# An order of steps for each engine in the attention stage of a decoder layer

## The chip, the cores and the metric

The kernel runs on one core of a Trainium2 chip, in one launch. Its engines work side by side, each through its own list of instructions: TensorE (PE, matmuls and transposes into PSUM), VectorE (DVE), ScalarE (ACT), GpSimd (POOL) and SyncE (SP), which starts most DMAs. They meet at semaphores: an instruction waits until a counter has reached a value, and everything behind it on the same engine waits too. The metric is the device time of the whole execution in microseconds.

## What is computed

One step of a two-layer decoder over 1024 prompt tokens and 8 x 4 sampled tokens. The first layer has a convolution branch and a sparse attention; the change lies in the attention. Cut to it:

```
def nsa_block(q, g, q_pos, kc, vc, kc_end, ks, vs, kw, vw, kw_pos):
    s_c = einsum('bqhgd,bnhd->bhgqn', qg, kc)          # compressed keys
    o_c = einsum(..., masked_softmax(s_c, ...), vc)
    ...                                                # scores of blocks, the best 16 are chosen
    s_s = einsum('bqhgd,bhqnd->bhgqn', qg, k_sel)      # selected keys
    o_s = einsum(..., masked_softmax(s_s, ...), v_sel)
    s_w = einsum('bqhgd,bwhd->bhgqw', qg, kw)          # window of 512 keys
    o_w = einsum(..., masked_softmax(s_w, ...), vw)
    return g0 * o_c + g1 * o_s + g2 * o_w
```

The prompt has 8 query tiles of 128 tokens and 2 key-value groups of 4 heads. For the samples the same is done over 2048 cached keys each, which are gathered from pages.

## The kernel before

**Units, pairs and turns.** The prompt's attention is cut into 48 units (query tile, group, branch), branch being PRS (selected), PRW (window) or PRC (compressed). Each unit has two pairs of heads, so 96 pairs. A pair goes through five steps on four engines: S, the scores (PE, L1137, 64 to 1024 keys, two rows of PSUM banks out of four); the row minimum with the mask (DVE, L1228, one instruction for each row); E, the exponential (ACT, L1177); the reciprocal of its sum (DVE, L1224); C, the scaling by that and by the gate (POOL, L1382). Then the unit's probabilities, 128 keys at a time, make 148 turns: T, four transposes into a PSUM bank (PE, L1151); a copy to one of two PT buffers (DVE L1165 or ACT L1168); V, the values (PE, L1024), which add up in bank 6. When a unit group of three branches is done, DVE multiplies it out (O, L1329).

**Work around them.** H is one of four subtractions of XL for the convolution half (DVE, L1334). The samples go through one PSUM bank, bank 7, in a chain of their own: scores over the compressed keys, a ranking of blocks (DVE, three steps for each of two halves, L1261 to L1269), and then, for each of four groups of two samples, gathers of keys (POOL, L1367), five rounds of key transposes (PE L1067, copied by ACT to KTS) and scores (PE L1072), two exponentials (ACT, L1191), two scalings (POOL, L1390), probability transposes (PE L1087 to L1092) and values (PE L1113). Each filling of bank 7 waits until the one before it has been taken out. The next group's gathers and window loads wait for the last values of a group. The loads of the output weights (SP, WOR) wait for the values of the last group; ACT rounds them (L1558) and POOL and DVE make the low part (L1562, L1570) before the output projection (PE, L1602).

**What sets the order.** One list, ORDER, is made by a loop that walks through the S and T steps with a rough clock, puts each E one S or T later and each C two later, and drops the sample steps in at given distances. Every engine walks through this one list and does what in it is its own. On PE the values of a turn come right behind the next S or T (flush). Copies are shared by the turn's number: even to DVE, odd to ACT. The steps H, the first gathers and the preparation (prep) are inserted at fixed places.

## Time and profile before

| | us |
|---|---|
| median of 3 runs | 1255.46 (1255.13 to 1256.18) |
| the profiled execution | 1259.05 |
| its span in the trace | 1257.3 |
| PE busy in the span | 1166.9 |
| DVE, ACT, POOL busy in the span | 751.5, 380.9, 330.7 |

A row of the trace gives the start, the duration, the engine, the line, what is written and read, and, in brackets, how long the engine stood idle before it and which instruction of which engine released it. The granted clock of PE is given as a share of 2.4 GHz; it knows two levels, 1.2 and 2.4 GHz, so 0.75 over a stretch means half of it at each.

### The profile page before, as it was taken

The page shows a single profiled execution, that of the slowest core. Times are in us where ns is not written, and L with a number is a line of the kernel's source. Part 1 is how long each engine was busy: PE and PEld are TensorE (multiplying, and loading weights), DVE is VectorE, ACT ScalarE, POOL GpSimd, SP SyncE. Part 2 cuts the span into 40 slices and gives each one's busy share as a digit, 9 for nine tenths or more (in the row PEclk, how much of TensorE's full clock was granted, in tenths as well). Part 3 has the DMA queues.
Part 4 walks back from the last instruction along what each step waited for, and adds up shares of the span by engine and source line. Part 5 has one row for each costly group of instructions (what it writes and reads, how often), then busy time and mean ns, then how long its engine had stood idle before and what let it go on. Part 6 is the DMA issues. An engine that isn't in the chain of part 4 may idle for free.

```text
span 1257.3 us, 17799 instructions
## 1 busy us (share of the span) xinstructions
PE 1166.9 (93%) x7124; PEld 939.9 (75%) x7124; DVE 751.5 (60%) x1381; ACT 380.9 (30%) x805; POOL 330.7 (26%) x340
## 2 busy tenths in 40 slices
PE   5888999999999688998999999889999999989997
PEld 4878999999889444554544545478879999988884
DVE  3566899998854686455355454484555660157555
ACT  3112111223124445545345455441011221234000
POOL 3443510000005654342333333340002221216000
PEclk9999999999999689799799999999999999999999
DMA  7553511433200400040040400272212111131221
GB/s 229 182 163 120 169 50 34 137 122 97 55 17 1 177 1 1 2 167 1 2 167 1 168 1 11 92 200 84 88 56 84 35 48 33 40 134 68 101 101 42
DMA packets 78011, 103.17 MB, mean 82 GB/s; under 512 B 21248, under 2 KB 64392, under 8 KB 76831
## 3 DMA queue, kind: packets, MB, share of 16 engines
q1 hardware_dynamic: 69839, 67.52, 17.3%
q0 software_dynamic: 6016, 33.56, 7.0%
q10 hardware_dynamic: 2080, 1.05, 0.3%
q8 instruction: 51, 0.84, 0.3%
q14 instruction: 25, 0.20, 0.1%
HBM read 90.42 MB, written 16.64 MB: 85 GB/s over the span
## 4 chain that ended last, share of the span: by engine, by line
PE 82%; DVE 8%; ACT 5%; issue 3%; POOL 2%; DMA 1%; SPq 0%; ACTq 0%; POOLq 0%
PE PS L681 24%; PE PS L1602 15%; PE PS L1764 14%; PE PS L1137 6%; PE PS L1024 5%; PE PS L1151 4%; PE PS L673 3%; PE PS L1113 2%; PE PS L1072 2%; DVE ACC L548 2%; PE PS L1067 1%; ACT PRW L1177 1%; PE PS L1744 1%; DVE PS L1228 1%; ACT PRS L1177 1%
## 5 line engine op out<-in xcount | busy, mean ns | idle before, releaser
L681 PE MATMUL PS<-XH,WH 128*128 128x352 f32 (+1 forms) x648 | 148.3, 333 | 3.1 <-DVE XL L523 3.1
L595 DVE SCALAR_TENSOR_TENSOR Y<-U,SM,Y 128x1024 f32<-128x1024 f32 x120 | 147.4, 1291 | 0.3
L681 PE MATMUL PS<-XH,WL 128*128 128x352 f32 (+1 forms) x648 | 143.0, 325 | 0.0
L681 PE MATMUL PS<-XL,WH 128*128 128x352 f32 (+1 forms) x648 | 142.9, 325 | 0.0
L681 PEld LDWEIGHTS PS<-XH,WH 128*128 128x128 f32 (+1 forms) x648 | 108.3, 187 | 6.5 <-DVE XL L523 3.8
L681 PEld LDWEIGHTS PS<-XL,WH 128*128 128x128 f32 (+1 forms) x648 | 109.8, 187 | 1.4
L681 PEld LDWEIGHTS PS<-XH,WL 128*128 128x128 f32 (+1 forms) x648 | 109.8, 186 | 1.4
L1024 PE MATMUL PS<-PT,TM 128*64 128x256 f32 x528 | 91.8, 428 | 12.2 <-ACT PT L1168 6.0
L548 DVE SCALAR_TENSOR_TENSOR ACC<-PS,SM,ACC 128x508 f32<-128x508 f32 x124 | 84.0, 739 | 30.7 <-PE PS L673 29.9
L1602 PE MATMUL PS<-WOH,XH 128*128 128x512 f32 (+1 forms) x288 | 91.4, 399 | 4.9 <-POOL WOL L1570 4.4
L1228 DVE CUSTOM_DVE_ANT_0 PS<-PS,MASKC 128x128 f32<-128x128 f32 (+7 forms) x96 | 62.6, 692 | 55.8 <-PE PS L1137 55.5
L1871 POOL TENSOR_TENSOR WL<-WRAW,WH 128x1024 fp32r<-128x1024 f32 x14 | 37.4, 2674 | 220.2 <-ACT WH L1816 220.2
L1137 PE MATMUL PS<-KV,Q 64*128 64x512 f32 (+3 forms) x384 | 87.3, 515 | 6.1 <-ACT PRS L1177 3.1
L290 POOL TENSOR_TENSOR WL<-WRAW,WH 128x1024 fp32r<-128x1024 f32 x12 | 28.6, 2386 | 244.4 <-ACT WH L362 244.4
L1602 PE MATMUL PS<-WOL,XH 128*128 128x512 f32 (+1 forms) x288 | 89.7, 393 | 0.0
L1602 PE MATMUL PS<-WOH,XL 128*128 128x512 f32 (+1 forms) x288 | 89.3, 391 | 0.0
L1382 POOL TENSOR_SCALAR PRS<-PRS,STAT,GTOK 128x128 f32<-128x128 f32 (+7 forms) x64 | 55.5, 878 | 96.5 <-DVE STAT L1224 96.3
L1165 DVE COPY PT<-PS 128x512 f32<-128x512 f32 x74 | 51.0, 689 | 50.1 <-PE PS L1151 49.3
L1764 PE MATMUL PS<-XH,WH 128*128 128x352 f32 x360 | 77.2, 323 | 0.0
L1764 PE MATMUL PS<-XH,WL 128*128 128x352 f32 x360 | 77.1, 323 | 0.0
L1764 PE MATMUL PS<-XL,WH 128*128 128x352 f32 x360 | 77.1, 323 | 0.0
L1137 PEld LDWEIGHTS PS<-KV,Q 64*128 64x128 f32 x384 | 38.9, 198 | 47.9 <-issue 26.1
(315 smaller groups left out, 2070.2 us busy)
## 6 DMA issues: line engine op xcount, KB each, us to landing
WRAW<-in_w_in_even SPq DMA_DIRECT2D x16, 512.0 KB
WRAW<-in_w_in_odd SPq DMA_DIRECT2D x16, 512.0 KB, 4.0
XIN<-in_x_prompt SPq DMA_DIRECT2D x8, 512.0 KB, 12.8
WRAW<-in_w_in_even SPq DMA_DIRECT2D x16, 256.0 KB
TM<-in_state_win_kv SPq DMA_DIRECT2D x8, 512.0 KB, 4.6
XR<-in_x_prompt SPq DMA_DIRECT2D x8, 512.0 KB, 3.5
layer_out<-R SPq DMA_DIRECT2D x8, 512.0 KB, 2.6
XR<-layer_out SPq DMA_DIRECT2D x8, 512.0 KB, 3.3
```

Of the source, the lines that this page charges most:

```text
L548: ins = v.scalar_tensor_tensor(acc, rows, weight, acc, ALU.mult, ALU.add)
L595: v.scalar_tensor_tensor(dst, src, CWT[:, i, t:t + 1], dst, ALU.mult, ALU.add).then_inc(s_cv, 1)
L673: ins = pe.transpose(PS[:, 6 + x, b * P:b * P + P], XC[:, load % 2, b, 256 * j + P * x:256 * j + P * x + P], ident[:, :])
L681: ins = pe.matmul(PS[0:mcols, 3 * slot + c, 0:CH], w[:, slot, kk, 0:mcols], x[:, kk, c * CH:(c + 1) * CH], start=(kk == 0 and n == 0), sto ...
L1024: ins = pe.matmul(PS[hb:hb + HD, 6, 256 * gp:256 * gp + 256], v, PT[0:rows, t % 2, 256 * h:256 * h + 256], start=first, stop=(br == CMPB))
L1137: ins = pe.matmul(PS[:, row_bank[j] + b // 512, 0:w], Q[hb:hb + HD, g, tok(qt)], keys[:, k0 + b:k0 + b + w], start=True, stop=True)
L1151: ins = pe.transpose(PS[0:cols, 4 + t % 2, c:c + P], probs(u, 2 * gl + h, i * P, cols), ident[:, :])
L1165: copy(PT[0:rows, t % 2, :], PS[0:rows, 4 + t % 2, :]).then_inc(sem, 1)
L1228: return v.tensor_tensor_reduce(out=out, in0=in0, in1=mask, scale=-SCALE, scalar=1e27, op0=ALU.add, op1=ALU.min, accum_out=acc)
L1382: po.tensor_scalar(x, x, RCP[:, stat(p, h):stat(p, h) + 1], GTOK[:, qt, c:c + 1], ALU.mult, ALU.mult)\
L1602: ins = pe.matmul(PS[0:n, b0 + hf, :], x[:, kk, tok(tt)], w[:, kk, hf * 512:hf * 512 + 512], start=(kk == 0 and i == 0), stop=(kk == KT - ...
L1764: ins = pe.matmul(PS[:, b0 + c, 0:CH], w[:, slot, kk, :], x[:, kk, c * CH:(c + 1) * CH], start=(kk == 0 and n == 0), stop=(kk == KT - 1 an ...
```

## The change

The list ORDER goes. Every step is declared with its engine, a kind, a duration in ns and the steps whose outputs it needs, and a planner lets simulated engines run: it takes again and again the step that can begin first, at equal times by the engine's order of kinds (URGENT), and appends it to that engine's own list.

```diff
-        for n, x in enumerate([("H", i) for i in range(4)] + [("gather", 0), ("prep",)]):
-            ORDER.insert(FIRST_H + 2 * n, x)
...
+        for p in range(NP):
+            u, n = p // 2, nkeys(p // 2)
+            step("PE", "S", ("S", p), 100 + 3.44 * n, *{("E", w // 2, w % 2) for w in row_waits[2 * p:2 * p + 2] if w >= 0})
+            for h in range(2):
+                step("DVE", "M", ("M", p, h), 180 + 1.13 * n, ("S", p))
+                step("ACT", "E", ("E", p, h), 250 + 0.84 * n, ("M", p, h), ("T", unit_last_turn[u - 3]) if u >= 3 else None)
+            step("DVE", "R", ("R", p), 170 if UNITS[u][2] != CMPB else 450, ("E", p, 1))
+            step("POOL", "C", ("C", p), 660 + 1.7 * n, ("R", p))
+        for t, (u, i) in enumerate(TURNS):
+            step("PE", "T", ("T", t), 520, ("C", 2 * u), ("C", 2 * u + 1), ("P", t - 2) if t >= 2 else None)
+            step("PE", "V", ("V", t), 550, ("P", t), ("O", u // 3 - 1) if u % 3 == 0 and i == 0 and u else None)
...
+            for k in range(3):
+                step("ACT", "X", ("sexp", gi, k), 1100 if k < 2 else 920, ("low", gi))
...
+            for k in range(2):
+                step("POOL", "X", ("sscale", gi, k), 810 if k else 2080, ("srec", gi))
...
+        URGENT = {"PE": "XSVT", "DVE": "PRMOQXH", "ACT": "PEX", "POOL": "CX"}
+        HANDOVER = 130
...
+            if kind == "T":
+                free = {c: max(now[c], end[what]) + ns * (1 + len(copies[c])) for c, ns in (("DVE", 690), ("ACT", 600))}
+                copier.append(min(("ACT", "DVE"), key=free.get))
+                copies[copier[-1]].append(what[1])
...
-            return (s_pted, t // 2 + 1) if t % 2 == 0 else (s_ptea, t // 2 + 1)
+            return s_pted if copier[t] == "DVE" else s_ptea, copier[:t + 1].count(copier[t])
...
+                    elif n == 1:
                         link(v.tensor_tensor(RE[:, :, :], RE[:, :, :], LT[:, :, :], ALU.mult))
-                    elif n == 1:
+                    elif n == 2:
                         link(v.tensor_tensor(RG[:, :, :], other, me, ALU.is_gt))
+                    elif n == 3:
                         link(v.tensor_tensor(RG[:, :, :], RG[:, :, :], RE[:, :, :], ALU.add))
...
-                    for i, t in enumerate((SS, SW)):
-                        act.activation(t[r, :], t[r, :], ACT.Exp, bias=ENM[r, 2 + i:3 + i], scale=-1.0,
-                                       accum_out=EDN[r, 2 + i:3 + i]).then_inc(s_eex, 1)
+                    half = (PAST + NSAMP) // 2
+                    t, i, total = ((SS[r, 0:half], 2, EDN[r, 2:3]), (SS[r, half:], 2, EDN2[r, :]), (SW[r, :], 3, EDN[r, 3:4]))[k]
+                    act.activation(t, t, ACT.Exp, bias=ENM[r, i:i + 1], scale=-1.0, accum_out=total).then_inc(s_eex, 1)
...
+                    link(v.tensor_tensor(EDN[r, 2:3], EDN[r, 2:3], EDN2[r, :], ALU.add))
```

So the minimum and the exponential of a pair's two rows become single steps; the values of a turn are a step of their own; a turn's copy goes to the engine that the planner finds free first, which gives DVE 49 and ACT 99 of the 148; the ranking has six steps for each half; the long exponential of a sample group is split in two, with an addition of the two sums; the two scalings of a group are two steps; and the four parts of a group's values stand one behind the other on PE. The first group's keys are taken 10 score steps and 9 turns later than before, and the last values of the last group come five turns before the end (turn 143 of 148, before 128).

At the start of the stage on DVE (ISA with MASKC is the minimum over a score row, XL the H step). Before:

```order
L1228 ISA PS,STAT<-PS,MASKC 128x128
L1228 ISA STAT 128x1
L1334 TENSOR_TENSOR XL<-Y,XH 128x1056 x2
L1224 RECIPROCAL STAT<-STAT 128x2
L1334 TENSOR_TENSOR XL<-Y,XH 128x1056
L1228 ISA PS,STAT<-PS,MASKC 128x128
```

After, at the same place:

```order
L1252 ISA PS,STAT<-PS,MASKC 128x128
L1252 ISA STAT 128x1
L1359 TENSOR_TENSOR XL<-Y,XH 128x1056
L1248 RECIPROCAL STAT<-STAT 128x2 x2
L1252 ISA PS,STAT<-PS,MASKC 128x128
```

Two H steps stood ahead of the first reciprocal, behind six score rows; now one stands ahead of the first two, behind four.

The start of the stage on POOL, from the last work of the convolution (XH) on. Before:

```order
L350 CAST XH<-Y 128x1056 x4
L1382 TENSOR_SCALAR PRS<-PRS,STAT,GTOK 128x128 x2
L1367 DMA RING<-in_cache_kv_sel,idx 128x4096 x2
L1382 TENSOR_SCALAR PRS<-PRS,STAT,GTOK 128x128 x2
L1432 IOTA TI 128x4
L1433 IOTA TI 128x1
L1435 MEMSET NEWM 128x64
L1436 AFFINE_SELECT NEWM<-NEWM 128x64
L1438 AFFINE_SELECT NEWM<-NEWM 128x64
L1440 MEMSET LT 128x900
L1441 AFFINE_SELECT LT<-LT 128x900
L1382 TENSOR_SCALAR PRW<-PRW,STAT,GTOK 128x128 x4
```

After:

```order
L350 CAST XH<-Y 128x1056 x4
L1409 TENSOR_SCALAR PRS<-PRS,STAT,GTOK 128x128 x4
L1409 TENSOR_SCALAR PRW<-PRW,STAT,GTOK 128x128 x4
L1409 TENSOR_SCALAR PRC<-PRC,STAT,GTOK 128x63 x4
L1409 TENSOR_SCALAR PRS<-PRS,STAT,GTOK 128x128 x4
L1409 TENSOR_SCALAR PRW<-PRW,STAT,GTOK 128x128 x4
L1394 DMA RING<-in_cache_kv_sel,idx 128x4096 x2
```

The gathers moved behind ten pairs, and the preparation (IOTA to the second LT row) behind fourteen.

ACT around the exponentials of the first sample group (SS, SW; PT is a turn's copy). Before:

```order
L1168 ACTIVATE PT<-PS 128x512
L1177 ACTIVATE PRS,STAT<-PS,STAT 128x512 x2
L1191 ACTIVATE SS,SE<-SS,SE 64x2080
L1191 ACTIVATE SW,SE<-SW,SE 64x544
L1168 ACTIVATE PT<-PS 63x512
L1177 ACTIVATE PRS,STAT<-PS,STAT 128x512 x2
```

After:

```order
L1195 ACTIVATE PT<-PS 128x512
L1202 ACTIVATE PRC,STAT<-PS,STAT 128x63
L1217 ACTIVATE SS,SE<-SS,SE 64x1040
L1195 ACTIVATE PT<-PS 128x512
L1217 ACTIVATE SS,SE<-SS,SE 64x1040
L1217 ACTIVATE SW,SE<-SW,SE 64x544
L1202 ACTIVATE PRS,STAT<-PS,STAT 128x640
```

A turn's copy now stands between the two halves of the long one in this group.

## Rows read from the trace of the kernel before

**Rows 1.** The page, second part: PE's granted clock in 40 slices, in tenths.

```profile
PEclk9999999999999689799799999999999999999999
```

**Rows 2.** Stretches: bounds, length, busy time of PE, PEld, DVE, ACT, POOL, clock, DMA.

```profile
410.68:816.05 405.37, 361.45 (x2449) 199.51 (x2448) 217.77 (x722) 195.84 (x539) 157.54 (x219) 0.92 0.16 61
410.68:436.87 26.19, 16.07 (x93) 10.39 (x92) 16.36 (x68) 10.68 (x48) 18.68 (x31) 0.61 0.56 213
410.68:500.00 89.32, 70.33 (x405) 38.73 (x406) 64.33 (x251) 44.61 (x168) 50.19 (x82) 0.81 0.17 63
500.00:816.05 316.05, 291.12 (x2046) 160.78 (x2042) 153.43 (x471) 151.22 (x371) 107.35 (x138) 0.95 0.16 61
```

**Rows 3.** Waits of PE in the stage: total, times, longest.

```profile
PE PS L1137 <- ACT PRW L1177: 8.6, 7, 3.1
PE PS L1024 <- DVE PT L1165: 6.9, 7, 1.5
PE PS L1024 <- ACT PT L1168: 6.8, 21, 1.7
PE PS L1072 <- ACT KTS L1168: 6.0, 15, 0.9
```

**Rows 4.** Timeline of PE: two turns' transposes at the lower clock and at full.

```profile
462.78 1.97 PE L1151 MATMUL PS<-ident,PRS 128*128 128x128 f32 x8
...
799.18 1.09 PE L1151 MATMUL PS<-ident,PRS 128*128 128x128 f32 x8
```

**Rows 5.** Stretches as in rows 2: those with a lowered clock, and the rest.

```profile
410.68:450.00 39.32, 27.98 (x151) 16.97 (x150) 26.22 (x125) 18.71 (x84) 25.51 (x45) 0.65 0.37 142
460.00:470.00 10.00, 8.34 (x35) 4.49 (x34) 7.60 (x29) 4.04 (x17) 5.52 (x8) 0.66 0.00 1
510.00:530.00 20.00, 19.23 (x100) 11.03 (x98) 8.37 (x32) 11.38 (x31) 10.46 (x14) 0.67 0.01 1
600.00:620.00 20.00, 18.14 (x105) 11.54 (x107) 5.19 (x22) 6.90 (x22) 7.91 (x10) 0.57 0.00 1
620.00:816.05 196.05, 182.78 (x1348) 100.51 (x1343) 98.79 (x283) 95.15 (x223) 65.87 (x80) 1.00 0.18 71
```

**Rows 6.** Timeline of PE: the first transposes of the first two turns.

```profile
424.25 1.11 PE L1151 MATMUL PS<-ident,PRS 128*128 128x128 f32 x4 [3.40 <-POOL PRS L1382]
...
429.28 1.12 PE L1151 MATMUL PS<-ident,PRW 128*128 128x128 f32 x4 [1.28 <-POOL PRW L1382]
```

**Rows 7.** Timeline of DVE and POOL at the start of the stage.

```profile
415.36 2.42 DVE L1334 TENSOR_TENSOR XL<-Y,XH 128x1056 fp32r<-128x1056 f32 x2
...
417.96 2.88 POOL L1382 TENSOR_SCALAR PRS<-PRS,STAT,GTOK 128x128 f32<-128x128 f32 x2 [3.04 <-DVE STAT L1224]
...
423.32 0.88 POOL L1382 TENSOR_SCALAR PRS<-PRS,STAT,GTOK 128x128 f32<-128x128 f32 x2
```

**Rows 8.** Timeline: a rank step of DVE, and the values of PE behind it.

```profile
456.15 1.33 DVE L1265 TENSOR_TENSOR RG<-RG,RE 128x900 f32<-128x900 f32 x1
...
459.05 0.65 PE L1024 MATMUL PS<-PT,VC 63*64 63x256 f32 x4 [0.86 <-DVE PT L1165]
```

**Rows 9.** Timeline: the second group's long exponential, and PE behind it.

```profile
591.76 2.02 ACT L1191 ACTIVATE SS<-SS,SE 64x2080 f32<-64x2080 f32 x1 [1.59 <-DVE SE L1277]
...
595.28 0.65 PE L1024 MATMUL PS<-PT,TM 128*64 128x256 f32 x4 [1.74 <-ACT PT L1168]
```

**Rows 10.** Last sample values, the loads behind them (KB, us to landing), the projection's start.

```profile
783.18 0.41 PE L1113 MATMUL PS<-VCN,TM 127*32 127x128 f32 x4
...
WOR<-in_w_out_even SPq DMA_DIRECT2D x4, 512.0 KB, 6.4
...
818.87 0.70 PE L1602 MATMUL PS<-WOH,XH 128*128 128x512 f32 x2 [2.82 <-POOL WOL L1570]
```

**Rows 11.** The gathers' line: from issue to landing.

```profile
DMA to landing us min/median/max: 8.9/11.5/14.6
```

**Rows 12.** Timeline of PE: a score step over 1024 keys.

```profile
785.73 1.99 PE L1137 MATMUL PS<-KV,Q 64*128 64x512 f32 x8
```

261 lines of the change are left out of this document (129 added, 132 removed).

## The prediction

> **What bounds the kernel now.** I read the page first, its busy rows in forty slices. TensorE (PE) is the fullest engine nearly everywhere, and its granted clock dips in only one part, slices 14 to 20 [rows 1]. That part is the attention stage, the only one that the change touches. The table by stretches gives its size: from the first scores at 410.68 to the last values at 816.05 it lasts 405.37 us, with PE busy for 361.45 us and idle for 43.9 us. DVE, ACT and POOL are busy for 217.77, 195.84 and 157.54 us of it, so none of them bounds the stage as a whole [rows 2]. The waits of PE in the stage name what it stood for: copies by ACT and DVE, mostly short (21 waits make 6.8 us), and exponentials in fewer and longer waits [rows 3].
>
> Busy time is not all work. The eight transpose records of two turns take 1.09 us at full clock and 1.97 us at the lower level of 1.2 GHz [rows 4], 1.81 times as long, so of what is done at the lower level 0.447 is excess. The mean clock in a stretch says how much of it lay at the lower level: 0.65 means 70%. Taken so, 19.6 us of the busy time up to 450, 5.7 us in 460 to 470, 12.7 us in 510 to 530 and 15.6 us in 600 to 620 were run at 1.2 GHz, and from 620 to the end none [rows 5]. That is 53.6 us, with 24.0 us of excess. So the stage is 337.4 us of PE work, 24.0 us of slow clock and 43.9 us of idling. Only the last two can go: the floor is 68 us below today's time.
>
> **The change, part by part.** The instructions stay the same but for four groups of small ones (below); what changes is who waits behind whom. Before, one list orders all engines; after, each has its own.
>
> *The start.* The first turn's transposes start at 424.25, after a wait of 3.4 us, and the second turn's at 429.28 [rows 6]. The chain behind them is on other engines: DVE subtracts two rows of XL (2.42 us from 415.36) before the first reciprocal, POOL then scales the first pair in 2.88 us instead of the 0.88 of the next, issues two gathers up to 423.3, scales the second pair and runs the preparation of the masks before the third [rows 7]. After, DVE has one XL row of half of 2.42 us before the first two reciprocals, and the gathers come behind ten pairs on POOL. That XL row can start about 1.1 us before today's 415.36, since two of the six score rows ahead of it, for which PE was waited, now stand behind (an estimate); it then ends at 415.5, the reciprocals at 415.8, four scalings of 0.44 us at 417.7; the next two pairs, one round of the same steps later, are scaled by about 420. So the first turn starts 6.4 us earlier and the second 9 us; I take **-7**, ends -5.5 and -9. What hides the rest of the XL rows is that nothing on PE needs them before the output projection, except through the gathers.
>
> The row of 2.88 us is POOL beside a DVE subtraction with both inputs in SBUF: 1.0 us lost for each scaling. From rows alone, POOL is idle for 248 of the stage's 405 us [rows 2] and the same instructions collide before and after, so I take 0 for such collisions, with +3 as an end. The Trainium skill, SBUF — State Buffer, section "Who interferes with whom", says that such a DVE instruction and a GpSimd one that reads SBUF exclude each other and that the second waits in full. By that rule, the trace agrees; and it speaks against the change, since three XL rows and eight of the twelve rank steps now stand among POOL's scalings, so that POOL would lose up to the length of each.
>
> *Rank steps.* DVE ran them in pairs. The second half of one, 1.33 us, ends at 457.5; the copy behind it is late and PE's values wait 0.86 us [rows 8]. After, each half stands alone. Between 436.87 and 500 PE idles 19.0 - 10.1 = 8.9 us [rows 2]. The early part also has DVE 72% busy (64.33 of 89.32 us), and the free choice of the copier takes 25 of DVE's 74 copies away, for ACT with 44.61 us busy [rows 2]. I take **-4** of the 8.9, ends -2 and -7.
>
> *Exponentials of the samples.* ACT was held by one of 2.02 us and a shorter one right behind; a copy due meanwhile came late, and PE's values waited 1.74 us [rows 9]. After, a copy or a pair's exponential can stand between three pieces of half that length. Of the 24.9 us of idling after 500 (316.05 - 291.12) I put 4 us on this: one such wait for each of four groups, less where PE had other work, and part of the 8.6 us for ACT's PRW, which stands behind the same block. The remaining waits are the short ones. With only half a turn between a turn's transposes and its values, the copy and its handovers are some 0.3 us too long (6.8 us in 21 waits). In the new order I count 18 turns with just one such piece between, against 27 before, so these shrink by a third; the waits between sample steps (6.0 us for L1072) keep their kind. With what the better places of the other copies bring I take -5 here, so **-9** after 500, ends -4 and -14.
>
> *Clock.* The two drops after 500 each come behind a block of ACT by the exponentials of a sample group (the second is the one shown), while from 620 on, with PE 93% busy, the clock stayed at full [rows 5]. Their excess is 0.447 x (12.7 + 15.6) = 12.7 us; I take **-10**, ends 0 and -12.7. The early excess is 0.447 x (19.6 + 5.7) = 11.3 us; the fill at the start stays, shorter by a third, so I take **-5.5**, ends 0 and -9.
>
> *Added.* Four more exponentials and four additions on DVE of a few hundred ns each (an estimate from the 0.44 us of the shortest scalings): they lie on the sample chain, which PE meets only at its end. **+0.5**, ends 0 and +2.
>
> *End of the stage.* The loads of the output weights wait for the last sample values. These ended at 783.6, 32 us before the stage's end; now some eleven pieces of 0.55 us and a wait or two follow, about 7 us. The loads land 6.4 us after their issue in the median, and ACT wants the first one some 6.3 us after it, when its last copy is done. They are just hidden: 0, with +2 as an end. The wait of 2.82 us at the start of the output projection stays [rows 10].
>
> *Gathers.* A sample group's gathers land after 8.9 to 14.6 us [rows 11]. Between its predecessor's last values and its first use stand five score steps (up to 2.0 us each) and 14 halves of turns, 12 to 15 us: covered, or short by 1 to 2 us in two or three groups, which is inside the ends above.
>
> The sum is -7 - 4 - 9 - 10 - 5.5 + 0.5 = **-35 us** against the profiled execution's 1259.05 us, so 1224. The median of the runs is 3.6 us lower than the profiled one, 1255.46, so I predict **1220 us**. With all favourable ends the sum is -52; the poor one (-5.5, -2, -4, a third of the clock, +2) is -15: its own range is 1204 to 1240.
>
> **Rivals.** (1) *The waits go, the clock stays low as long as before.* All of -19.5 comes, nothing of -15.5: 1236. For it: the start remains a fill, and 18 short waits remain. Against it: 620 to 816 has 13 us of idling in short waits and a clock of 1.00 throughout [rows 5]. The Trainium skill has a rule for this, TensorE: Matmul & The Clock Gate, section "A second HAM failure mode: psum-queue depth-cycling": frequent short idling between groups of matmuls makes the clock go to and fro.
>
> (2) *The planned order is wrong in detail.* Its table prices a score step at 3.44 ns per key and pair, 3.6 us for 1024 keys; the row shows 1.99 us [rows 12]. Engines keep their order however early a step's input is there, so a copy planned behind an exponential may come late, and each saved wait returns elsewhere. Then only the start and the split exponentials are left, about -10: 1245. Against it: between two wide score steps PE must wait for both exponentials anyway, about 4.2 us, and the planner leaves as much for other work.
>
> (3) *Slower: short waits everywhere bring the clock down.* Same mechanism as (1), going further: turns now come as two transposes and two values, with about 0.3 us of idling in a pair. It decides from the point where the busy time at 1.2 GHz passes 53.6 + 19.5/0.447 = 97 us. With a third of the 337 us of work there, it takes 0.81 x 112 = 91 us longer than at full clock, where today's excess is 24; less the 19.5 us of waits that is 48 us slower, about 1303. Against it is again the stretch from 620, where such pairs stand already.
>
> **Chances.** Forecast 0.74, (1) 0.12, (2) 0.06, (3) 0.06, no change for unseen reasons 0.02. A measurement tells about 0.2% (2.5 us) from no change. Faster 0.91, same 0.03, slower 0.06. The range reaches over (1) and half of (2): 1203 to 1243, with some 2 in 10 outside.
>
> **What would show it.** First transposes at about 418 and second at 420; the stage some 370 us long with at most 25 us of PE idling; the clock at 1.00 from about 440 on, with no drop at the sample exponentials; DVE with about 49 copies. It would be wrong if the clock stays below 0.95 over the stage, if PE waits more for copies than 14 us in all, or if the output projection starts more than 4 us behind the last values.

## The result, and the profile after

The kernel after takes 1201.39 us (median of 4 runs, 1198.82 to 1204.59) against 1255.30 us before (4 runs, 1250.78 to 1256.18): ratio 0.958, 95% interval 0.9549 to 0.9611. The direction was as forecast; the size was not. The forecast was -35 us, and it came out as -54, beyond the lower end of the range at 1203. The profiled executions, 1259.05 and 1204.59 us, differ by 54.5 us.

The page of the kernel after, second part: PE's granted clock in 40 slices (before: rows 1).

```profile
PEclk9899999999999979999999999899999999999999
```

One lowered slice is left in the stage; a slice is 30 us. The stage runs from the first scores at 412.64 to the last values at 762.35. The view by stretches has the columns of rows 2.

```profile
412.64:762.35 349.71, 330.08 (x2449) 191.88 (x2448) 203.44 (x701) 208.61 (x572) 158.08 (x219) 0.98 0.18 68
412.64:500.64 88.00, 78.68 (x483) 44.19 (x482) 69.95 (x284) 55.77 (x205) 59.03 (x95) 0.90 0.18 64
500.64:762.35 261.71, 251.40 (x1970) 147.69 (x1966) 133.49 (x417) 152.83 (x367) 99.05 (x125) 1.00 0.18 69
762.35:1202.90 440.55, 422.29 (x2258) 375.06 (x2256) 228.90 (x296) 88.90 (x138) 78.34 (x29) 0.98 0.26 82
```

Against [rows 2] the stage is 55.7 us shorter. What follows it takes 440.55 us; before it was 1257.3 - 816.05 = 441.25. What lies ahead of it ended 2.0 us later. So the whole difference is in the stage: -55.7 + 2.0 - 0.7 = -54.4 us, as the spans say. The same number of matmuls, 2449, stands in both stages.

The stage can be cut into three, as the prediction did, here with the clock of each slice of 10 us for both kernels: idle time, the low clock's excess (0.447 of what was run at the lower level), and the rest, which I call **work at full clock**.

| stage, us | length | idle | excess of the low clock | work at full clock |
|---|---|---|---|---|
| before | 405.4 | 43.9 | 23.8 | 337.7 |
| after | 349.7 | 19.6 | 6.8 | 323.3 |
| difference | -55.7 | -24.3 | -17.0 | **-14.4** |
| forecast | -35 | -20 | -15.5 | 0 |

The forecast's -35 has 0.5 us more for the added instructions. Idle time and clock are near the forecast. The last column is what was missed: with the same instructions, PE was busy for 14 us less, clock apart. The waits of PE that are left (total, times, longest; before: rows 3):

```profile
PE PS L1056 <- ACT PT L1195: 7.8, 17, 1.2
PE PS L1165 <- ACT PRW L1202: 3.3, 5, 1.2
PE PS L1179 <- POOL PRS L1409: 1.8, 2, 0.9
PE PS L1094 <- DMA RING<-in_cache_kv_sel,idx: 1.5, 2, 0.9
PE PS L1069 <- DVE QBD L1441: 1.2, 1, 1.2
PE PS L1056 <- DVE BG L1354: 1.0, 2, 0.6
PE PS L1056 <- DVE PT L1192: 0.9, 4, 0.3
```

No wait is over 1.2 us, where [rows 3] had one of 3.1 us. The largest total is now that of values (L1056) for a turn's copy by ACT; before it was that of scores for the exponentials.

### The profile page after: what moved, and what is told of

Same layout as the page of the kernel before. It is cut to its first block, busy times and chain, and to the rows that moved or that the text cites. A ratio compares the mean times of both kernels' runs of the same rounds, so it can differ in the third digit from the quotient of the medians.

```text
span 1202.9 us, 17825 instructions
## 1 busy us (share of the span) xinstructions
PE 1138.5 (95%) x7124; PEld 934.8 (78%) x7124; DVE 734.9 (61%) x1360; ACT 394.8 (33%) x838; POOL 330.4 (27%) x340
## 4 chain that ended last, share of the span: by engine, by line
PE 83%; DVE 8%; DMA 4%; ACT 3%; POOL 1%; issue 1%; SPq 0%; ACTq 0%; POOLq 0%; DVEq 0%
PE PS L681 25%; PE PS L1629 17%; PE PS L1791 14%; PE PS L1165 5%; PE PS L1056 5%; PE PS L1179 4%; PE PS L673 3%; DMA RING<-in_cache_kv_sel,idx 2%; PE PS L1140 2%; PE PS L1094 2%; DVE ACC L548 2%; PE PS L1099 2%; DVE PS L1252 1%; PE PS L1771 1%; DMA idx<-in_page_table 1%
## 5 line engine op out<-in xcount | busy, mean ns | idle before, releaser
L1056 PE MATMUL PS<-PT,TM 128*64 128x256 f32 x528 | 82.3, 407 | 9.9 <-ACT PT L1195 7.8
L1165 PE MATMUL PS<-KV,Q 64*128 64x512 f32 (+3 forms) x384 | 78.5, 498 | 0.4 <-ACT PRS L1202 0.3
L1195 ACT ACTIVATE PT<-PS 128x512 f32<-128x512 f32 (+1 forms) x99 | 59.0, 597 | 55.7 <-PE PS L1179 55.4
L1679 DVE SCALAR_TENSOR_TENSOR R<-XR,PS 128x1024 f32<-128x1024 f32 (+1 forms) x18 | 21.9, 1219 | 81.3 <-PE PS L1629 81.3
## 6 DMA issues: line engine op xcount, KB each, us to landing
XIN<-in_x_prompt SPq DMA_DIRECT2D x8, 512.0 KB, 12.7
```

The costliest lines, as they stand in the source:

```text
L1056: ins = pe.matmul(PS[hb:hb + HD, 6, 256 * gp:256 * gp + 256], v, PT[0:rows, t % 2, 256 * h:256 * h + 256], start=first, stop=(br == CMPB))
L1165: ins = pe.matmul(PS[:, row_bank[j] + b // 512, 0:w], Q[hb:hb + HD, g, tok(qt)], keys[:, k0 + b:k0 + b + w], start=True, stop=True)
L1195: copy = lambda o, i: act.activation(o, i, ACT.Copy)
```

## Where busy time hid a wait

A score step (L1137 before) issues the matmuls of two heads in turn. Each head waits inside the step, before its own first matmul, for the exponential that frees its banks. The timeline of PE in the kernel before has these two neighbours:

```profile
596.19 2.12 PE L1137 MATMUL PS<-KV,Q 64*128 64x512 f32 x8 [0.26 <-ACT PRS L1177]
...
600.06 2.12 PE L1137 MATMUL PS<-KV,Q 64*128 64x512 f32 x8 [1.18 <-ACT PRW L1177]
```

Both are steps over 640 keys. Another one over 640 keys, the same eight matmuls, takes less in the same trace:

```profile
792.59 1.35 PE L1137 MATMUL PS<-KV,Q 64*128 64x512 f32 x8
```

A step of 1.35 us has both heads' matmuls side by side; in one of 2.12 us the first head began when its bank was free, and the second came later. The profile names only the wait ahead of the first matmul, and counts what lies between the heads as busy. Single records bear it out: in the steps of 1.35 us the second head's first matmul starts 0.01 us after the first head's, in one of 1.57 us it is 0.23 us, in those of 2.12 us 0.78 us. So the step is longer by about what the second head is late. The reading was tested by putting both waits ahead of the step.

### Both waits ahead of a score step, in before and after

The edit is the same in both kernels:

```diff
                     k0, nk = P * key_tiles(u)[0], nkeys(u)
+                    if max(row_waits[2 * p:2 * p + 2]) >= 0:
+                        pe.wait_ge(s_exp, max(row_waits[2 * p:2 * p + 2]) + 1)
                     for b in range(0, nk, 512):
...
-                            if b == 0 and row_waits[j] >= 0:
-                                pe.wait_ge(s_exp, row_waits[j] + 1)
```

> The kernel before, with one edit: a score step waits for the exponentials that free both of its rows' banks before its first matmul, where before it began the first row as soon as that one's bank was free. Theory A (part of PE's busy time in the kernel before was waiting inside score steps, which the records count as work, since the two heads' matmuls run side by side only when both may start): 640-key steps of 2.12 us turn into 1.35 us with an idle time ahead of them; PE busy in the stage falls by 5 to 8 us, idle rises by as much, the time stays within 3 us of 1255. Theory B (a score step's busy time is work and does not depend on the wait): busy time stays at 361 us within 2, idle rises by the full wait for the second exponential, about 1 us for each of some 20 steps, and the time rises by 10 to 20 us.

Measured: 1259.03 us (1252.57 to 1262.02, 10 runs) against 1255.23, ratio 1.0023 (0.9998 to 1.0049). The stage as a stretch, and its longest waits of PE:

```profile
412.23:819.01 406.78, 352.02 (x2449) 192.69 (x2448) 217.03 (x722) 195.91 (x539) 158.17 (x219) 0.92 0.16 61
```

```profile
PE PS L1137 <- ACT PRW L1177: 14.9, 11, 3.6
PE PS L1137 <- ACT PRS L1177: 8.1, 8, 2.5
```

Busy time fell by 9.4 us and idle time rose by 10.9. The time is 3.8 us up by the medians, which the interval doesn't tell from no change; theory B's 10 to 20 us are excluded. Theory A stands, with more hidden than its 5 to 8 us. The waits of score steps for the exponentials rose from 8.6 us for PRW [rows 3] and 3.1 for PRS to 23.0. So of the 337.7 us of "work" some 9.6 were waiting: 328.1 us are left. Then the same in the kernel after:

> The kernel after, with one edit: a score step waits for the banks of both its rows before its first matmul, as in the same edit of the kernel before, where 9.4 us of TensorE's busy time in the stage turned into idle time. The stage of the kernel after is 349.7 us, 330.1 of it busy, and its busy time less the low clock's excess is 11 to 14 us under that of before. Theory A (before held some 9 us of waiting inside its score steps, and the planned order holds almost none): busy falls by no more than 4 us (to 326 or more), the waits of score steps for the exponentials (3.3 us) rise to at most 8, and the time stays within 4 us, 1199 to 1205. So 5 us or more of the 11 to 14 are these waits gone. Rival (both orders hold as much, and the gain in busy time is all from steps of one kind that stand together): busy falls by 8 to 10 us, to 321, those waits rise to 12 or more, and the time stays as well or rises to 1206 to 1210.

Measured: 1199.75 us (1197.15 to 1200.68, 4 runs) against 1255.98, ratio 0.9545 (0.9507 to 0.9582).

```profile
409.46:756.88 347.42, 323.35 (x2449) 185.16 (x2448) 203.91 (x701) 207.21 (x571) 157.89 (x219) 0.99 0.18 69
```

Work at full clock is 319.9 us, 3.4 less than in after. Waits for exponentials became 4.7 + 3.0 us, from 3.3. So the planned order removed 9.6 - 3.4 = 6.2 us of waiting that the profile of before shows as busy time. The time is like that of after: theory A.

## Steps of one kind together

After the edit above, no score step waits between its heads, and the two orders still differ: 328.1 against 319.9 us, 8.2 us. Rows of the kernel after show what could make this: two turns' values that stand one behind the other, and a single one.

```profile
736.65 0.65 PE L1056 MATMUL PS<-PT,TM 128*64 128x256 f32 x4 [0.35 <-ACT PT L1195]
737.24 1.09 PE L1179 MATMUL PS<-ident,PRS 128*128 128x128 f32 x8
...
740.06 1.08 PE L1056 MATMUL PS<-PT,TM 128*64 128x256 f32 x8
741.08 0.44 PE L1165 MATMUL PS<-KCT,Q 64*128 64x63 f32 x4
```

Rows that follow each other without a wait overlap by some 0.07 us, so it is the starts that count: behind the single one the next row starts after 0.59 us, behind the pair after 1.02. The pair saves 0.15 us against two single ones. The order of after has two values steps together in 32 places (before in 1), two transposes in 38 (27), and its PE changes from one kind of step to another 394 times (451); these are counts of the order of steps, with the samples' steps as one kind.

### Strict alternation, without and with the waits ahead

Values of turn t - 2 must stand ahead of the transposes of t, and transposes of t + 1 ahead of the values of t.

```diff
-            step("PE", "T", ("T", t), 520, ("C", 2 * u), ("C", 2 * u + 1), ("P", t - 2) if t >= 2 else None)
-            step("PE", "V", ("V", t), 550, ("P", t), ("O", u // 3 - 1) if u % 3 == 0 and i == 0 and u else None)
+            step("PE", "T", ("T", t), 520, ("C", 2 * u), ("C", 2 * u + 1), ("V", t - 2) if t >= 2 else None)
+            step("PE", "V", ("V", t), 550, ("P", t), ("T", t + 1) if t + 1 < len(TURNS) else None, ("O", u // 3 - 1) if u % 3 == 0 and i == 0 and u else None)
```

> The changed kernel, but its planner must alternate turns: the values of turn t come behind the transposes of t+1, and the transposes of t+2 behind those values (no two value steps and no two transpose steps stand together; 32 and 38 did). Theory A (each change between transposes and values costs PE 0.06 to 0.07 us, since two together take 1.02 to 1.04 us and a single one 0.58): busy time in the stage rises by 4 to 5 us over the 330 of the changed kernel, waits for copies fall by up to 6, the time is 1198 to 1205. Theory B (PE's work is the same in any order): busy stays at 330 within 1.5, waits fall by 4 to 6 us, the time falls to 1195 or so.

Measured: 1207.19 us (1205.48 to 1208.60, 4 runs) against 1255.23, ratio 0.9615 (0.959 to 0.964). Changes of kind rose to 462.

```profile
412.67:764.98 352.31, 340.24 (x2449) 190.97 (x2448) 188.22 (x672) 224.56 (x601) 156.04 (x219) 0.97 0.18 71
```

Idle time fell to 12.1 us, the lowest of all these kernels, with 0.6 us in waits of values for ACT's copies; and yet the stage is longer than in after, since PE is busy for 10 us more: 7.0 of work at full clock and 3.1 of the low clock's excess. Both theories had the time too low, and theory A had the busy time's rise at 4 to 5 us. This kernel could itself hold more waits inside its score steps, so it was run with these ahead as well.

> The kernel after with two edits: strict alternation of a turn's transposes and an earlier turn's values (alone: 1207.2, busy time less the low clock's excess 331.1 us in the stage, against 324.2 in after), and the waits for the banks of both rows ahead of each score step (alone: 1199.8, 320.5 us). Theory A (the 6.9 us between alternation and after are what changes between kinds of steps cost; the waits inside score steps are about the same few us in both): the edit takes 2 to 5 us out, 326 to 329 us stay, 6 us or more above the 320.5 of after with the same edit; time 1204 to 1209. Rival H (the alternating order holds more waits inside score steps, and changes of kind cost nothing): 9 to 11 us go, 320 to 322 us stay, the waits of score steps for the exponentials rise by as much; time the same or 1 to 3 us up.

Measured: 1205.16 us (1202.78 to 1206.95, 4 runs) against 1258.19, ratio 0.9588 (0.9539 to 0.9637).

```profile
407.49:761.18 353.69, 336.74 (x2449) 185.17 (x2448) 187.06 (x672) 224.82 (x601) 156.01 (x219) 0.97 0.18 70
```

| work at full clock, us | waits inside the steps | waits ahead | changes of kind on PE |
|---|---|---|---|
| before | 337.7 | 328.1 | 451 |
| after, strictly alternating | 330.3 | 327.2 | 462 |
| after | 323.3 | 319.9 | 394 |
| after, score price 2.6 (below) | 323.0 | 320.5 | 408 |
| after, copies by parity (below) | 319.6 | not run | 363 |

With no waits inside steps, alternation gives 7.3 us of the 8.2 back. Theory A stands: the 14.4 us are 6.2 us of waiting inside score steps and some 7 to 8 us for like steps that stand together, about 0.1 us for each change of kind (7.3 us for 68 changes). The last two rows are not made for this question: the one has 14 changes more than after and 0.6 us more work where 1.5 were to be expected, the other 31 fewer and 3.7 us less. So the price of a change is known to no better than some hundredths of a us.

The records of the three kernels with the waits ahead, each counted up to the start of the next, say where the 8.2 us between before and after lie: 5.0 in the values of the turns (88.0 to 83.0 us), 2.4 in their transposes (83.7 to 81.3) and 1.7 in the values of the samples, whose four parts now stand together, with about 1 us lost in other steps. Alternation brings 3.9 and 4.4 us of values and transposes back. In part the cost goes with the shape of the matmuls. From the start of a turn's four transposes to the start of the next step it is 0.58 us if values or scores follow, and 0.49 us if the samples' key transposes do, or if the two stand the other way round, as in the rows below. Both of these are 128*128 (the first figures of a row); values and scores are not.

```profile
707.46 0.66 PE L1094 MATMUL PS<-ident,RING 128*128 128x128 f32 x4
707.95 0.60 PE L1179 MATMUL PS<-ident,PRS 128*128 128x128 f32 x4
```

This also shows that idle time alone is no aim: the order with 7.5 us less of it was 5.8 us slower by the medians, all four of its runs above the four of after, and 2.6 us in the stages of the two traces.

## The parts of the change, alone in the kernel before

The start: the H steps, the first gathers and the preparation put behind later steps of the shared list.

```diff
-        for n, x in enumerate([("H", i) for i in range(4)] + [("gather", 0), ("prep",)]):
-            ORDER.insert(FIRST_H + 2 * n, x)
-        ORDER.insert(FIRST_H + 40, ("prep2",))
+        def put(x, after):
+            ORDER.insert(ORDER.index(after) + 1, x)
+
+        put(("H", 0), ("S", 1))
+        put(("H", 1), ("S", 5))
+        put(("H", 2), ("S", 9))
+        put(("H", 3), ("S", 10))
+        put(("gather", 0), ("C", 9))
+        put(("prep",), ("C", 12))
+        put(("prep2",), ("C", 13))
```

> The kernel before with only the start reordered as in the change: one XL subtraction ahead of the first reciprocals and the other three later, the first gathers behind the tenth pair's scaling, the mask preparation behind the thirteenth. Theory A (the prediction's start term): first transposes 5 to 7 us after their place in the changed kernel's trace relative to the stage's start, that is 8 us into the stage instead of 13.6, 7 us faster for the waits and up to 6 more for the clock. Theory B (the first 40 us are bound by DVE, whose work is only moved): 0 to 4 us faster, since the idling comes back by 500.

Measured: 1255.39 us (1250.75 to 1258.31, 10 runs) against 1255.23, ratio 0.9991 (0.997 to 1.0012), no gain, as theory B allowed. The first transposes came 7.8 us into the stage and the second 11.8 (before 13.57 and 18.60 [rows 6]); but PE idled 3.3 us less, not 6 to 7. The view of waits has a new line:

```profile
PE PS L1063 <- DVE TM L1260: 4.8, 1, 4.8
```

The samples' exponentials cut into three. The edit gives each group 2 us more in the rough clock that makes the list, so that the chain's later steps slip too: 137 turns stand ahead of its last values, 128 before.

```diff
-                       (("low", gi), 0, 0), (("sexp", gi), 500, 0), (("srec", gi), 2500, 0), (("sscale", gi), 0, 0)]
+                       (("low", gi), 0, 0), (("sexp", gi, 0), 500, 0), (("sexp", gi, 1), 1500, 0), (("sexp", gi, 2), 1500, 0), (("srec", gi), 1500, 0), (("sscale", gi), 0, 0)]
...
+                    half = (PAST + NSAMP) // 2
+                    t, i, total = ((SS[r, 0:half], 2, EDN[r, 2:3]), (SS[r, half:], 2, EDN2[r, :]), (SW[r, :], 3, EDN[r, 3:4]))[k]
```

> The kernel before with only the sample exponentials split: the long one in two halves and the window one as steps of their own, with other work of the list between them, and one addition of the two sums. Theory A (the blocks of 2.8 us on ACT cause both the waits behind them and the drops of the clock at 510 to 530 and 600 to 620): both drops go, clock over the stage 0.96 instead of 0.92, 10 to 17 us faster than before. Theory B (the drops come from the short idling all around or from the narrow matmuls of the sample steps that follow): at least one of the drops stays, 0 to 6 us faster.

Measured: 1252.20 us (1247.71 to 1255.90, 10 runs) against 1255.23, ratio 0.9974 (0.9954 to 0.9994). The excess of the low clock fell from 23.8 to 11.0 us, idle time rose from 43.9 to 47.8. PE's largest total of waits is now for the other engine's copies (6.9 us before [rows 3]):

```profile
PE PS L1025 <- DVE PT L1166: 11.2, 17, 2.0
```

Theory A had 10 to 17 us and both drops gone, theory B a drop that stays and 0 to 6 us; the time is B's. The drop at 600 to 620 is gone, of that at 510 to 530 the first half is as it was (0.84), and a new one stands at 690 to 710. Nor is all of the trace's 12.8 us a gain: this execution has the highest clock of its ten (0.981, their median is 0.976), the profiled one of before with 0.967 a low one (median 0.971). So the block has a part in the clock, and the drops have other causes besides, which stay open. The waits do not go; that each turn's copy keeps its engine by parity and its place in the shared list is the likely reason. Both parts together:

> The kernel before with two parts of the change at once: the rank moved out of the start (alone it gave 1255.4, ratio 0.9991) and the samples' exponentials cut into three (alone 1252.2, ratio 0.9974). Order and copying engines of everything else stay as they are. Theory A (the parts are worth little by themselves, since the waits that they remove come back as waits for other work that keeps its place in the hand-made order; only an order for each engine collects them): the sum of the two, 1249 to 1255, idle time in the stage 40 to 48 us, and the waits of values for copies made by VectorE stay above 8 us. Rival C (the two hold each other back, by the clock: each leaves one stretch at the low level): together they bring the clock to 1.00 from 450 us on, the low clock's excess falls to 10 us or less, and the time is 1238 to 1247.

Measured: 1249.09 us (1247.60 to 1253.85, 10 runs) against 1255.98, ratio 0.9954 (0.993 to 0.9977). In this case the two are not worth more together than the sum of their parts, within the runs' spread; idle time is 43.4 us as before. Theory A stands, by its waits too, which stay for copies made by DVE:

```profile
PE PS L1032 <- DVE PT L1173: 10.7, 17, 2.0
```

The low clock's excess is 15.9 us, so rival C is out. So of 54 us these two parts bring some 3 to 7 without the planned order. The other parts were not tried in the hand-made list, the free copier above all; that the rest needs an order for each engine is argued from the waits that came back, not shown.

## The parts taken out of the kernel after

Each of these undoes one part; the planner knows of it and plans anew. First the copies by parity again (DVE 74 in place of 49):

```diff
-                copier.append(min(("ACT", "DVE"), key=free.get))
+                copier.append(("DVE", "ACT")[what[1] % 2])
```

> The changed kernel with the copies shared by parity again (even turns DVE, odd ACT), the plan made with that: DVE has 74 copies instead of 49. Theory A (the free choice is worth something only in the first 90 us, where DVE is 80% busy): waits there rise by 3 to 6 us, nothing after, 1203 to 1209. Theory B (an engine order that is planned for parity hides it too): within 2 us of 1201. Theory C (the free choice is the main part of the gain): above 1215.

Measured: 1213.34 us (1211.27 to 1214.23, 4 runs) against 1251.82, ratio 0.9671 (0.9627 to 0.9715), between theories A and C, 12 us above after by the medians, 11 by the ratios, and the intervals are clear of each other. Waits of values for DVE's copies are 9.5 us and long ones are back, two waits for gathers grew, and the clock falls at 490 and at 570 besides:

```profile
PE PS L1056 <- DVE PT L1192: 9.5, 17, 1.7
PE PS L1094 <- DMA RING<-in_cache_kv_sel,idx: 4.4, 2, 3.3
```

Its stage is 10.4 us longer than that of after: 8.8 of idling and 5.3 of low clock, less 3.7 of work. This is the largest of the single parts. Next, the two rows of a pair as one step again:

```diff
...
-            for h in range(2):
-                step("DVE", "M", ("M", p, h), 180 + 1.13 * n, ("S", p))
-                step("ACT", "E", ("E", p, h), 250 + 0.84 * n, ("M", p, h), ("T", unit_last_turn[u - 3]) if u >= 3 else None)
+            step("DVE", "M", ("M", p, 1), 360 + 2.26 * n, ("S", p))
+            step("ACT", "E", ("E", p, 1), 500 + 1.68 * n, ("M", p, 1), ("T", unit_last_turn[u - 3]) if u >= 3 else None)
...
```

> The changed kernel with the minimum and the exponential as steps of a pair (both rows in one) in the plan and on the engines, as before the change. Theory A (single rows let a copy slip in between two exponentials, and that is where the waits for copies and the waits inside score steps went): PE's waits for copies rise from 9 to 15 us or more and PE busy rises by 2 to 5 us through waits inside score steps, 1207 to 1216. Theory B (the planner's times do the work, whatever the size of a step): within 3 us of 1201.

Measured: 1206.24 us (1204.06 to 1207.52, 4 runs) against 1251.82, ratio 0.9615 (0.9571 to 0.966): +4.9 by the medians, between the two theories. The waits for ACT's copies are 7.7 us, as in after, so theory A's mechanism is out. What rose in its trace are waits for gathers, 5.2 us, and for scalings of the selected branch, 3.9 us, and the low clock's excess, 10.6 us from 6.8. Then the samples' exponentials as one block of three in a single step:

```diff
-                step("ACT", "X", ("sexp", gi, k), 1100 if k < 2 else 920, ("low", gi))
+                if k == 2:
+                    step("ACT", "X", ("sexp", gi, k), 3120, ("low", gi))
...
```

> The changed kernel with each sample group's exponentials as one block of 2.8 us on ACT again. Theory A (the block causes the waits behind it and a drop of the clock, wherever it stands): PE waits 1 to 2 us behind each of four blocks and the clock falls behind at least one, 1206 to 1216. Theory B (a planner that knows its length puts it where PE has other work): within 3 us of 1201, clock 1.00 from 450 on.

Measured: 1205.99 us (1202.19 to 1206.98, 4 runs) against 1251.82, ratio 0.961 (0.9564 to 0.9657): +4.6 by the medians. The longest wait for a copy is 2.6 us and the clock stays at 1.00 from 450 on. So in the planned order a block of 2.8 us no longer goes with a drop of the clock, as in before, which is theory B's part; that it stands where PE has other work is the likely reason. Whether this kernel and the one before it lose at all against after is not shown: their intervals overlap that of after (0.9549 to 0.9611), and the kernel before, run beside them, had a median of 1251.82 in place of 1255.30.

## The price of a score step

The prediction's second rival had it that the table's 3.44 ns a key is wrong, since the trace shows 1.99 us for 1024 keys [rows 12]. It was tried:

```diff
-            step("PE", "S", ("S", p), 100 + 3.44 * n, *{("E", w // 2, w % 2) for w in row_waits[2 * p:2 * p + 2] if w >= 0})
+            step("PE", "S", ("S", p), 100 + 1.87 * n, *{("E", w // 2, w % 2) for w in row_waits[2 * p:2 * p + 2] if w >= 0})
```

> The changed kernel with the planner's price of a score step at 1.87 ns per key, as the trace shows for steps that do not wait inside, instead of 3.44. Theory A (the wrong price misplaces steps, the prediction's second rival): waits fall, 1193 to 1199. Theory B (the order is not sensitive to it, because a later score step waits for both exponentials anyway): within 3 us of 1201. Theory C (the high price leaves slack that real handovers need, so that the true one plans too tight): waits for exponentials rise, 1204 to 1212.

Measured: 1225.01 us (1223.23 to 1226.90, 4 runs) against 1251.82, ratio 0.9772 (0.9726 to 0.9817). None of the theories had this. The stage in stretches:

```profile
407.25:726.70 319.45, 307.72 (x2266) 176.78 (x2265) 192.73 (x674) 201.03 (x556) 155.13 (x217) 0.98 0.17 68
727.00:785.00 58.00, 28.72 (x183) 15.46 (x182) 6.96 (x24) 13.97 (x23) 5.32 (x4) 0.62 0.16 60
```

The stage begins at 407.25 here and the prompt's last values end at 726.7, 319.5 us later where it is 349.7 in after, with 11.7 us of idling. But the samples' chain is not done: by the plan all 148 turns stand ahead of its last values (143 in after), and for 58 us it runs alone, with PE half idle and three quarters of the stretch at the low clock (0.62). Its waits in the timeline of PE:

```profile
726.73 0.66 PE L1094 MATMUL PS<-ident,RING 128*128 128x128 f32 x4
728.08 0.66 PE L1094 MATMUL PS<-ident,RING 128*128 128x128 f32 x4 [0.69 <-ACT KTS L1195]
...
736.69 1.12 PE L1094 MATMUL PS<-ident,RING 128*128 128x128 f32 x4 [0.81 <-DVE LOW L1252]
738.49 1.11 PE L1094 MATMUL PS<-ident,RING 128*128 128x128 f32 x4 [0.69 <-ACT KTS L1195]
...
762.80 1.08 PE L1114 MATMUL PS<-ident,SS 64*128 64x64 f32 x8 [6.49 <-POOL SS L1417]
...
785.02 1.19 PE L1629 MATMUL PS<-WOH,XH 128*128 128x512 f32 x2 [9.31 <-POOL WOL L1597]
```

The prices do not only describe the steps: they set how fast the plan thinks the prompt's rows go, and so how many of the chain's steps it puts among them. In the next kernel the chain was let forward in the rankings (DVE "PRMXOQH", ACT "PXE"), at the same price.

> The kernel after, with three edits of the planner alone: a score step costs 100 + 1.87 ns a key in place of 3.44 (which gave 1225.0 by itself, with the sample chain's last step put behind all 148 turns and 58 us from there to the projection), and to keep that chain up, its steps stand ahead of the minima in VectorE's ranking of kinds and ahead of the exponentials in ScalarE's. In the plan 122 turns now stand ahead of the chain's last step (143 in the kernel after, all 148 with the price alone). Theory D (the price alone lost its time only in the tail, where the chain ran alone at the low clock): the tail is gone, the stage ends some 345 to 352 us after it starts, and the time is 1196 to 1203; if the idle time of the first 314 us (9.4 us, against 19.6 in the stage of after) is kept as well, the lower end. Rival E (a score price near the trace's own makes the plan too tight: rows run ahead, the sample steps take VectorE and ScalarE from the rows as soon as they are let forward): idle time of TensorE above 25 us, waits of transposes or values for the engines behind them, 1206 to 1215.

Measured: 1209.48 us (1207.42 to 1212.18, 4 runs) against 1255.98, ratio 0.9634 (0.9596 to 0.9673). The tail is gone, but the stage is 357.9 us with 23.0 us of idling, and one wait is new:

```profile
PE PS L1056 <- DVE BG L1354: 8.1, 1, 8.1
```

The timeline of DVE has six rank steps in a row ahead of that write (four of them here):

```profile
457.34 1.10 DVE L1285 TENSOR_TENSOR RE<-TM 128x900 f32<-128x900 f32 x1
458.47 1.28 DVE L1287 TENSOR_TENSOR RE<-RE,LT 128x900 f32<-128x900 f32 x1
459.78 1.10 DVE L1289 TENSOR_TENSOR RG<-TM 128x900 f32<-128x900 f32 x1
460.91 1.10 DVE L1291 TENSOR_TENSOR RG<-RG,RE 128x900 f32<-128x900 f32 x1
...
463.65 0.42 DVE L1354 TENSOR_TENSOR BG<-PS,BG 128x256 f32<-128x256 f32 x1
```

A rank step is ranked above the output's write there, and six of them held PE for 8.1 us; in 500 to 520 the clock was 0.74 besides. So the time is rival E's, and so is the mechanism, in this one place; its idle time of 25 us is not reached. Last came a price between, with X and Q exchanged in DVE's ranking and X ahead of E in ACT's. The exchange has no effect: run with DVE's ranking of after, the planner makes the same list for every engine, so that DVE's ranking is in effect that of after.

```diff
-            step("PE", "S", ("S", p), 100 + 3.44 * n, *{("E", w // 2, w % 2) for w in row_waits[2 * p:2 * p + 2] if w >= 0})
+            step("PE", "S", ("S", p), 100 + 2.6 * n, *{("E", w // 2, w % 2) for w in row_waits[2 * p:2 * p + 2] if w >= 0})
...
-        URGENT = {"PE": "XSVT", "DVE": "PRMOQXH", "ACT": "PEX", "POOL": "CX"}
+        URGENT = {"PE": "XSVT", "DVE": "PRMOXQH", "ACT": "PXE", "POOL": "CX"}
```

> The kernel after, with two edits of the planner alone: a score step costs 100 + 2.6 ns a key (3.44 in after, 1.87 in the two others), and the sample steps stand ahead of the exponentials in ScalarE's ranking. VectorE's ranking is that of after. With 1.87 and the chain ahead of the minima the time was 1209.5: six pieces of the rank stood on VectorE from 457.3 to 463.4 us ahead of the write of a finished output, TensorE waited 8.1 us for that one, and the clock fell in the stretch from 500 to 520. In this plan 136 turns stand ahead of the sample chain's last step (143 in after, 148 with 1.87 alone). Theory D (the price is right as long as the chain keeps up and no rank stands ahead of an output's write): no wait above 2 us, idle time in the stage 14 to 19 us, clock 1.00 behind 450, stage 342 to 347 us, and 1194 to 1199. Rival F (the 3.44 of after is a good price just because the plan then leaves slack that the other engines use up): idle time 20 us or more in waits for copies by ScalarE, 1201 to 1208.

Measured: 1197.40 us (1194.99 to 1202.17, 6 runs) against 1255.95, ratio 0.9528 (0.9501 to 0.9555).

```profile
412.17:759.02 346.85, 329.76 (x2449) 189.04 (x2448) 196.47 (x693) 213.25 (x580) 156.15 (x219) 0.98 0.19 72
```

Idle time is 17.1 us, the longest total wait for one cause is 8.1 us in 18 pieces of at most 1.8 us, and the clock is 1.00 behind 450: theory D in every point. It has the lowest median of the kernels, 4 us under that of after; the intervals of the two ratios just overlap (0.9555 and 0.9549), so that it beats after is likely and not shown. The price by itself would not do it: with 2.6 and ACT's ranking of after the planner puts all 148 turns ahead of the chain's last values again (no run of that). With the waits for both rows' banks ahead as well:

> The kernel after with the score price of 2.6 ns a key and the sample steps ahead of the exponentials in ScalarE's ranking (alone 1197.4), and the waits for both rows' banks ahead of each score step (alone 1199.8 where after has 1201.4). Theory A (a wait inside a score step costs the same as one ahead of it, since the second head's matmuls only run by themselves instead of beside the first's, which is little dearer): busy time falls by 3 to 7 us, idle time rises by as much, the time stays at 1195 to 1200. Rival (a step whose two heads start together is over sooner, so that waiting ahead is a gain by itself): 1192 to 1195.

Measured: 1197.67 us (1195.18 to 1198.84, 4 runs) against 1258.19, ratio 0.9521 (0.9473 to 0.9568). Theory A: where the wait stands changes what the profile calls busy (326.4 against 329.7 us), not the time.

## Why the forecast was too small

**The step that failed** is in the first part: "the stage is 337.4 us of PE work, 24.0 us of slow clock and 43.9 us of idling. Only the last two can go." Busy time less the slow clock was taken as fixed because the instructions are the same. The runs showed 14.4 us of it to go: 6.2 us were waits between the two heads of score steps, and 7 to 8 us came from fewer changes of kind. The trace of before showed the first already: a step over 640 keys took 2.12 us in some rows and 1.35 us in others, at full clock. I used one row of the score steps for a price and did not compare equal steps with each other. With -14.4 in the sum it is -49, and with the idle time (-24.3 in place of -20) and the clock (-17.0 in place of -15.5) as measured it is the stage's -55, of which 1.3 us were lost outside the stage.

**The start, -7, and the rank, -4.** The first transposes stand 7.3 us into the stage (419.98 less 412.64) and the second turn's 10.2 us:

```profile
419.98 1.12 PE L1179 MATMUL PS<-ident,PRS 128*128 128x128 f32 x4
...
422.83 1.12 PE L1179 MATMUL PS<-ident,PRW 128*128 128x128 f32 x4
```

That is 6.2 and 8.4 us earlier, where I had 6.4 and 9. POOL's first four scalings took 1.75 us, what four of 0.44 make, with a DVE subtraction of XL (1.99 us from 415.99, where I had 1.2) just over when they began at 418.17. Up to 500 (89.3 and 88.0 us of stage) the idle time fell from 19.0 to 9.3 us: -9.7 for both terms together, against -11. The two terms cannot be told apart in after; alone in the hand-made order the start was worth nothing, so that its -7 is not shown as a term of its own.

**After 500, -9.** Idle time went from 24.9 to 10.3 us, -14.6, just past my end of -14. The term was a little too small, and its split was not right: to the exponentials of the samples I gave 4 us and to all better places of the copies 5. With the exponentials as one block again the idle time of the whole stage is 20.7 us, 1.0 above after. The run with copies by parity says that the free choice of the copier carries more than that, +12 us when undone; its idle time after 500 is 16.2 us, 5.9 above after. In the timeline of ACT of after, a copy stands between the halves of the long exponential, as the order said:

```profile
521.15 1.16 ACT L1217 ACTIVATE SS<-SS,SE 64x1040 f32<-64x1040 f32 x1
...
522.29 0.58 ACT L1195 ACTIVATE PT<-PS 128x512 f32<-128x512 f32 x1
522.77 1.16 ACT L1217 ACTIVATE SS<-SS,SE 64x1040 f32<-64x1040 f32 x1
```

**Clock, -10 and -5.5.** It came to -17.0 us. From 450 to the stage's end the clock is 1.00, so both late drops went with all their excess (12.7 us), and the early one fell by about 4.3. That the drops come behind ACT's block is shown in part: with that block cut in before, the one at 600 to 620 went, half of the other stayed, and a new one came. With 17 waits for ACT's copies of at most 1.2 us left, the clock stayed at full; the rule of the Trainium skill, TensorE: Matmul & The Clock Gate, section "A second HAM failure mode: psum-queue depth-cycling", by which frequent short idling makes it go to and fro, is not borne out by this stage. Where PE stood for 0.69 or 0.81 us ahead of each of its steps, as in the tail of the kernel with the price of 1.87, the clock did fall, and stayed low. How much idling brings it down, the runs don't tell. Rivals (1) and (3) fell.

**Collisions of POOL and DVE, 0.** POOL is busy for 158.08 us in the stage, before 157.54. So the sum of what it loses beside DVE hardly changed, as assumed.

**End of the stage and gathers, 0.** The output projection waits 3.12 us for the output weights, against 2.82 [rows 10], and two waits for gathers make 1.5 us. Both inside the ends.

**Rival (2).** It rightly asked what the price of 3.44 ns does, and its answer was wrong twice. With another price and ranking some 4 us were to be had, no more; and with the price nearest to the trace's the time goes up by 24 us, 8 with the chain of the samples kept up.

The range ended at 1203 because all its favourable ends were bounds on idle time and clock. A bound on the work itself was missing: with it the range would have begun at about 1190.

## What to carry to other kernels

Before a busy time is called a floor, compare equal steps of the engine with each other at the same clock: where one takes 2.12 us and its twin 1.35, there is a wait inside, and a wait ahead of the step makes it visible, here at no cost that the runs could tell. In this hand-made order for all engines two single improvements hardly paid, and waits came back at other fixed places; the order for each engine with a free copier had both the short waits and the full clock. And a planner's prices are levers as much as measurements: a change of price has to be read at the end of the plan, where the chain that it put off comes due.

## What the runs showed of the hardware

Score matmuls with 64 rows for two heads ran side by side when both could start: 1.35 us together, 2.12 us when the second head began 0.78 us late. Changing between kinds of steps on TensorE cost about 0.1 us each in this stage, 7.3 us for 68 changes, though no engine was waited for. Part of it goes with a change of the matmuls' shape (0.58 us from start to start, 0.49 where the neighbour has the same 128*128); what takes the rest, the runs don't tell. And a chain that had TensorE to itself, waiting 0.69 or 0.81 us between steps of 1 to 2 us, ran at the low clock: a transposition of four tiles took 1.12 us there, 0.66 at its start.
